# Value and gate projections of the second layer as seven block products instead of eight

## What is computed

```python
def odd_layer(x, w_in, w_gk2, b_gk, g_norm, w_out):
    h = x @ w_in                                  # (1024, 1024) @ (1024, 3088)
    q, k, v, gk_low, g = _split(h, ODD_SPLITS)    # 512, 512, 1024, 16, 1024
    o = gla_layer(q, k, v, gk_low, w_gk2, b_gk, g_norm) * jax.nn.silu(g)
    return o @ w_out
...
x = layer_norm(DEEPNORM_ALPHA * x + y, ln_g[layer], ln_b[layer])
```

## Time and profile before

| | |
|---|---|
| median of three runs | 904.2 us (903.74 to 906.98) |
| profiled execution | 907.0 us, of which the profile's span is 905.3 |
| TensorE busy | 870.0 us (96%), 4456 matmuls |
| VectorE busy | 473.1 us (52%) |
| ScalarE busy | 283.5 us (31%) |
| GpSimd busy | 253.7 us (28%) |
| moved by DMA | 55.8 MB |

### The profile page before, as it was taken

The page is one execution under the profiler, slowest core; times in us unless marked ns, Lnnn a source line. Parts: engine busy times, 40 slices in busy tenths (PEclk is TensorE's granted clock), DMA queues, the critical chain, the costliest instruction groups (busy, mean ns, idle before and its releaser), DMA issues. The chain is left out here.

```text
span 905.3 us, 12067 instructions
## 1 busy us (share of the span) xinstructions
PE 870.0 (96%) x4456; PEld 708.6 (78%) x4456; DVE 473.1 (52%) x805; ACT 283.5 (31%) x554; POOL 253.7 (28%) x275
## 2 busy tenths in 40 slices
PE   7999999999899999999997999999999999999995
PEld 5889877766677877787875888888888888888884
DVE  5988698556787786637852634000000127545553
ACT  6251514653234334412324453001102145211220
POOL 2000001424211202307655430133323323232243
PEclk9999999999999999999998999999999999999998
DMA  9110165210000201033314110211011332121111
GB/s 326 39 28 20 47 116 103 60 55 1 1 2 1 70 2 47 1 117 113 119 69 142 47 47 0 63 55 47 12 36 47 96 126 82 42 76 47 46 58 60
DMA packets 35050, 55.80 MB, mean 62 GB/s; under 512 B 7744, under 2 KB 21312, under 8 KB 34976
## 3 DMA queue, kind: packets, MB, share of 16 engines
q1 hardware_dynamic: 34992, 55.03, 20.2%
HBM read 43.94 MB, written 9.44 MB: 59 GB/s over the span
## 5 line engine op out<-in xcount | busy, mean ns | idle before, releaser
L1596 DVE SCALAR_TENSOR_TENSOR w_out_lo<-w_out_raw,vecs,w_out_hi 128x1024 fp32r<-128x1024 f32 x8 | 10.3, 1285 | 162.0 <-ACT w_out_hi L1186 161.8
L1887 PEld LDWEIGHTS psum<-V,probT 128*128 128x128 f32 x576 | 69.3, 192 | 12.5 <-issue 8.6
L1887 PE MATMUL psum<-V,probT 128*128 128x64 f32 x576 | 74.5, 275 | 0.5 <-DVE rot L1539 0.3
L1750 PE MATMUL psum<-kT,qTt 96*128 96x512 f32 (+3 forms) x192 | 72.9, 490 | 1.2 <-DVE YT L626 1.2
L1101 ACT ACTIVATE prob<-psum,negmax 128x128 f32<-128x128 f32 (+7 forms) x64 | 47.4, 741 | 82.1 <-DVE negmax L1478 74.4
L1478 DVE TENSOR_REDUCE negmax<-psum 128x1 f32<-128x128 f32 (+7 forms) x64 | 48.5, 758 | 29.5 <-PE psum L1754 28.0
L1663 PE MATMUL psum<-x1T_hi,wqk_hi 128*128 128x512 f32 x128 | 51.0, 398 | 0.0
L1663 PE MATMUL psum<-x1T_lo,wqk_hi 128*128 128x512 f32 x128 | 50.8, 397 | 0.0
L1663 PE MATMUL psum<-x1T_hi,wqk_lo 128*128 128x512 f32 x128 | 50.8, 397 | 0.0
L1663 PE MATMUL psum<-w_out_hi,Y1T_hi 128*128 128x512 f32 x128 | 50.6, 395 | 0.0
L1663 PE MATMUL psum<-w_out_hi,Y1T_lo 128*128 128x512 f32 x128 | 49.9, 390 | 0.0
(11 more groups left out here) (360 smaller groups left out, 2046.0 us busy)
## 6 DMA issues: line engine op xcount, KB each, us to landing
wqk_raw<-odd_w_in_dram SPq DMA_DIRECT2D x8, 512.0 KB, 5.4
x_res<-x_dram SPq DMA_DIRECT2D x8, 512.0 KB, 4.2
x_scratch<-zn SPq DMA_DIRECT2D x8, 512.0 KB, 2.9
wv_raw<-odd_w_in_dram SPq DMA_DIRECT2D x16, 256.0 KB, 2.7
wg_raw<-odd_w_in_dram SPq DMA_DIRECT2D x16, 256.0 KB, 2.7
w_out_raw<-odd_w_out_dram SPq DMA_DIRECT2D x4, 1024.0 KB, 4.9
V<-x_scratch SPq DMA_DIRECT2D x8, 512.0 KB, 4.2
out_dram<-SG SPq DMA_DIRECT2D x8, 512.0 KB, 2.9
```

The source lines that it names most:

```text
L1596: step(vec.scalar_tensor_tensor(w_out1[2][:, k, :], w_out1[0][:, k, :], gla_c[:, 4 + k % 2:5 + k % 2], w_out1[1][:, k, :].bitcast(F32), AL ...
L1750: mm = pe.matmul(psum[:, slot + part, 0:c1 - c0], qTt[:, i % 2, h, :], kT[:, h, c0:c1], start=True, stop=not diag, skip_group_check=diag)
L1887: mm = pe.matmul(bank("o", i)[:, h * VD:(h + 1) * VD], lhsT, rhs, start=(k == 0), stop=(k == len(pairs) - 1))
```

## The change

v1 and g1 become seven products of half-size blocks each, by Strassen's identity in the form with few additions. The 1024 tokens and 1024 channels of the input and the channels and columns of the weights are cut in halves. A11 and A12 multiply input blocks by plain weight blocks and gather in one bank; the other five (S2, S3, A22, S1, S4) take sums and differences of input blocks or of weight blocks. One product of one of v1 and g1 is 4 channel blocks ("slices") x 4 token tiles x 3 matmuls of the same shape as before; there are 56 slices, numbered 0 to 55, v1 and g1 in turn for each product. For each slice 1 to 4 pieces of 256 KB are loaded (`PIECES`) into one of three slots, and GpSimd and VectorE subtract them: two pieces GpSimd alone, three GpSimd then VectorE, four GpSimd twice, then VectorE. ScalarE makes the hi part, VectorE the lo part; only the first four slices are still split by GpSimd.

The sums of input blocks (`sum_raw`, `s2_raw`, `x1_lo_raw`) are made once: six instructions of 2048 columns on GpSimd, three after k1 of m = 5 and three after k1 of m = 7, and 16 of 512 columns on VectorE; ScalarE and VectorE split them again. The products are put together in V1 and SG: ScalarE copies A11 and A11 + A12 out, VectorE adds the other five onto it, and Silu runs in place on ScalarE. VectorE and ScalarE have a list of 60 rounds ("tick"), one per slice and four behind. `w_out1` is loaded and split in halves of 512 columns, the load of `ln_gb` is moved behind the stage, and its place is used by one of the slots. The memset of `att` moves into round 46, and the two semaphores of the output stores become one.

The core of the diff:

```diff
+        sum_raw = at("sum_raw", RD + 4096, [P, 4, 512])
...
+        vg_raw = [[at(f"vg{s}_raw{j}", a, [P, 512]) for j, a in enumerate(slot[:4])] for s, slot in enumerate(vg_at)]
+        vg_hi = [at(f"vg{s}_hi", slot[4], [P, 512], F32R) for s, slot in enumerate(vg_at)]
+        vg_lo = [at(f"vg{s}_lo", slot[5], [P, 512], F32R) for s, slot in enumerate(vg_at)]
...
+        A11, A12, S2, S3, A22, S1, S4 = range(7)
+        PIECES = {A11: ((0, 0),), A12: ((1, 0),), S2: ((1, 1), (0, 1), (0, 0)), S3: ((1, 1), (0, 1)),
+                  A22: ((1, 0), (1, 1), (0, 1), (0, 0)), S1: ((0, 1), (0, 0)), S4: ((1, 1),)}
+        ADDS_TO = (A12, A22, S4)
+        NVG = 56
+
+        for product in range(7):
+            for name in ("v1", "g1"):
+                for t in range(4):
+                    ring(name, product, t)
...
+        def vg_slice(n):
+
+            step_, k = divmod(n, 4)
+            return step_ // 2, ("v1", "g1")[step_ % 2], k
...
+        first_rows, last_rows = slice(0, 512), slice(512, S)
+        row_parts = {A11: (slice(0, 4), first_rows), A12: (slice(4, 8), first_rows), S3: (slice(0, 4), last_rows),
+                     A22: (slice(4, 8), last_rows), S1: (slice(4, 8), first_rows), S4: (slice(0, 4), first_rows)}
...
+        ROW_SUMS = (S2, S3, S1, S4)
...
+            def vg_load(n):
+
+                if n >= 7:
+                    sp.wait_ge(vg_split, n - 6)
+                product, name, k = vg_slice(n)
+                base = {"v1": 2 * GKW, "g1": c_gk + GR}[name]
+                for j, (r, c) in enumerate(vg_pieces(n)):
+                    sp.dma_start(vg_raw[n % 3][j][:, :], w_in1[r * 512 + k * P:r * 512 + (k + 1) * P,
+                                                               base + c * 512:base + (c + 1) * 512]).then_inc(
+                        vg_loaded[n % 3], 16)
...
+            plan.filled(sp, ("k1", 2 * GH - 1))
+            sp.wait_ge(qk_set, 2 * GH)
+            for n in range(4, NVG):
+                vg_load(n)
+                if n == 45:
+                    plan.filled(sp, ("g1", A22, 3))
+                    w_out1_load(0, 0, 1)
+                    w_out1_load(0, 4, 1)
+                if n == 53:
+                    plan.filled(sp, ("g1", S1, 3))
+                    w_out1_load(1, 4, 0)
+            plan.filled(sp, ("g1", S4, 3))
+            w_out1_load(2, 0, 0)
+            for n, w in enumerate((ln_g, ln_b)):
+                sp.dma_start(ln_gb[:, n, :], w[1:2, :].partition_broadcast(P)).then_inc(ln1_loaded, 16)
...
+            plan.filled(pool, ("k1", 5))
+            upper, lower = (slice(None), slice(0, 4), last_rows), (slice(None), slice(4, 8), last_rows)
+            step(pool.tensor_tensor(sum_raw[:, :, :], x1T_hi[upper].bitcast(F32), x1T_hi[lower].bitcast(F32), ALU.add))
+            step(pool.tensor_tensor(s2_raw[:, :, :], x1T_lo[upper].bitcast(F32), x1T_lo[lower].bitcast(F32), ALU.add))
+            step(pool.tensor_tensor(sum_raw[:, :, :], sum_raw[:, :, :], s2_raw[:, :, :], ALU.add), s1_s3_set)
+
+            plan.filled(pool, ("k1", 2 * GH - 1))
+            corner = (slice(None), slice(0, 4), first_rows)
+            step(pool.tensor_tensor(x1_lo_raw[upper], x1T_lo[corner].bitcast(F32), x1T_lo[upper].bitcast(F32), ALU.subtract))
+            step(pool.tensor_tensor(x1_hi_raw[upper], x1T_hi[corner].bitcast(F32), x1T_hi[upper].bitcast(F32), ALU.subtract))
+            step(pool.tensor_tensor(x1_lo_raw[upper], x1_lo_raw[upper], x1_hi_raw[upper], ALU.add), s1_s3_set)
+
+            for n in range(4, NVG):
+                q, *p = [raw[:, :] for raw in vg_raw[n % 3]][:len(vg_pieces(n))]
+                if p:
+                    pool.wait_ge(vg_loaded[n % 3], vg_landed(n))
+                if len(p) == 1:
+                    step(pool.tensor_tensor(q, q, p[0], ALU.subtract), vg_pool_sum)
+                elif len(p) == 2:
+                    step(pool.tensor_tensor(p[0], p[0], p[1], ALU.subtract), vg_pool_sum)
+                elif len(p) == 3:
+                    step(pool.tensor_tensor(p[1], p[1], p[2], ALU.subtract))
+                    step(pool.tensor_tensor(p[0], p[0], p[1], ALU.subtract), vg_pool_sum)
...
+            def vg_round(n):
+
+                if n >= 7:
+                    vg_done(act, n - 3)
+                if len(vg_pieces(n)) == 1:
+                    act.wait_ge(vg_loaded[n % 3], vg_landed(n))
+                elif len(vg_pieces(n)) == 2:
+                    act.wait_ge(vg_pool_sum, vg_pool_sums(n))
+                else:
+                    act.wait_ge(vg_vec_sum, vg_vec_sums(n))
+                step(act.activation(vg_hi[n % 3][:, :], vg_raw[n % 3][0][:, :], ACT.Copy), vg_hi_set)
...
+            def product_out(name, product, t):
+
+                job, dst = (name, product, t), {"v1": V1, "g1": SG}[name]
+                if product in (A11, A12):
+                    plan.filled(act, job)
+                    cols = first_rows if product == A12 else last_rows
+                    step.frees(act.activation(dst[:, t, cols], bank(*job),
+                                              ACT.Silu if name == "g1" and product == A12 else ACT.Copy), job)
+                elif name == "g1" and product in (A22, S1, S4):
+                    plan.drained(act, job)
+                    z = {A22: SG[:, 4 + t, first_rows], S1: SG[:, 4 + t, last_rows], S4: SG[:, t, last_rows]}[product]
+                    step(act.activation(z, z, ACT.Silu))
...
+            for tick in range(2, NVG + 4):
+                if tick + 2 < NVG:
+                    vg_round(tick + 2)
+                for first, product in ((8, S2), (17, S3), (21, S1), (25, S4)):
+                    if first <= tick < first + 4:
+                        rows_round(product, tick - first)
+                if tick >= 4:
+                    product, name, t = vg_slice(tick - 4)
+                    product_out(name, product, t)
+                if 48 <= tick < 56:
+                    w_out1_hi(tick - 48, 1)
+                if 56 <= tick < 60:
+                    w_out1_hi(tick - 52, 0)
...
+            def vg_low(n):
+
+                vec.wait_ge(vg_hi_set, n - 3)
+                step(vec.tensor_tensor(vg_lo[n % 3][:, :], vg_raw[n % 3][0][:, :], vg_hi[n % 3][:, :].bitcast(F32),
+                                       ALU.subtract), vg_split)
+
+            def vg_sum(n):
+
+                if len(vg_pieces(n)) >= 3:
+                    vec.wait_ge(vg_pool_sum, vg_pool_sums(n))
+                    q, p = vg_raw[n % 3][0][:, :], vg_raw[n % 3][1][:, :]
+                    step(vec.tensor_tensor(q, q, p, ALU.subtract), vg_vec_sum)
...
+            def product_sum(name, product, t):
+
+                job, dst = (name, product, t), {"v1": V1, "g1": SG}[name]
+                if product in (A11, A12):
+                    return
+                plan.filled(vec, job)
+                if product == S2:
+                    plan.drained(vec, (name, A11, t))
+                right, below = dst[:, t, last_rows], dst[:, 4 + t, last_rows]
+                out_, with_ = {S2: (right, right), S3: (below, right), A22: (dst[:, 4 + t, first_rows], right),
+                               S1: (below, below), S4: (right, right)}[product]
+                ins = vec.tensor_tensor(out_, with_, bank(*job), ALU.add)
+                step.frees(ins, job)
+
+            vec.wait_ge(s1_s3_set, 1)
+            for tick in range(NVG + 4):
+                if 4 <= tick + 2 < NVG:
+                    vg_low(tick + 2)
+                if 4 <= tick + 3 < NVG:
+                    vg_sum(tick + 3)
+                if tick < 4:
+                    k = tick
+                    step(vec.tensor_tensor(s2_raw[:, k, :], sum_raw[:, k, :], x1T_hi[:, k, first_rows].bitcast(F32), ALU.subtract))
+                    step(vec.tensor_tensor(s2_raw[:, k, :], s2_raw[:, k, :], x1T_lo[:, k, first_rows].bitcast(F32), ALU.subtract),
+                         s2_s4_set)
+                if 8 <= tick < 12:
+                    k = tick - 8
+                    if k == 0:
+                        plan.filled(vec, ("g1", A11, 3))
+                        vec.wait_ge(s1_s3_set, 2)
+                    s4 = x1_lo_raw[:, k, first_rows]
+                    step(vec.tensor_tensor(s4, x1T_hi[:, 4 + k, first_rows].bitcast(F32), s2_raw[:, k, :], ALU.subtract))
+                    step(vec.tensor_tensor(s4, s4, x1T_lo[:, 4 + k, first_rows].bitcast(F32), ALU.add), s2_s4_set)
+                for first, product in ((12, S2), (17, S3), (21, S1), (25, S4)):
+                    if first <= tick < first + 4:
+                        rows_low(product, tick - first)
+                if tick >= 4:
+                    product, name, t = vg_slice(tick - 4)
+                    product_sum(name, product, t)
+                if tick == 46:
+                    step(vec.memset(att[:, :, :, :], 0.0))
+                if 49 <= tick < 57:
+                    w_out1_lo(tick - 49, tick - 49, 1)
+                if 57 <= tick < 60:
```

(31 more changed lines are left out.)

164 lines of the change are left out of this document (83 added, 81 removed).

## The result

The changed kernel takes 921.4 us (median of four runs, 919.03 to 926.27) against 904.2 us before: ratio 1.0188, 95% interval 1.0125 to 1.0251. It is slower; whether by more than 2% the interval leaves open. A fourth run of the kernel before, in the same session, fell in a slow state (992.4 us) and is not counted. The profiled execution took 919.03 us, its span 917.0, against 907.0 and 905.3.

What follows compares the result with a forecast made beforehand. It took TensorE, busy throughout the value and gate projections, as the bound; −21.8 + 5.6 + 2.5 + 4.0 + 9.8 + 2.7 = +2.8 us gave 909.8 profiled, 907.0 median. Likeliest case 897 to 916; 8-in-10 range 892 to 918.

Steps and rivals of the forecast that it cites:

- step 1: Start of the stage: TensorE waits at slice 4 for VectorE's low part, held by wide GpSimd sums; 5.6 us.
- late starts in the stage: Matmuls at low clock behind the wait at slice 4: one fall to 1.2 GHz, 2.5 us.
- step 2: Products S2 and S3: VectorE's rounds 13 to 28 take longer than TensorE's slices, partly covered; 4.0 us.
- step 3: Product A22, four pieces per slice: GpSimd and VectorE strictly in turn, 3.95 us per slice against 2.72; 9.8 us.
- step 4: End of the stage: ScalarE and VectorE pass gate tiles between them, so key-value matmuls start later; 2.7 us.
- B: Rival: the clock falls again in A22 and stays at 1.2 GHz, 9.4 us more, 916 us; chance 0.12.
- S3's second condition: Start of S3: its first matmuls also need the last S2 product sum; no separate size given.
- load chain: A22: a slot is loaded again only after its low part, 10.1 us for three slices, 3.4 each.
- A: Rival: the shared port decides less, GpSimd subtracting in VectorE's pauses; 890 to 898, say 894 us; chance 0.21.
- C: Rival: GpSimd–VectorE hand-overs cost instead of saving, A22 at 5.0 us per slice; 919 us; chance 0.08.
- D: Rival: the stage isn't shortened, matmuls coming further apart with four banks sharing a slice; chance 0.02.
- high end: Whole kernel: all added costs at their upper bounds, 33.8 us, giving 916 us.

Runs made afterwards that it cites:

- e1: Changed kernel with GpSimd's six wide sums of input blocks each made as four of 512 columns: 914.7 us, ratio 1.0100.
- e7: e1 with VectorE's eight subtractions on the rows of S2 made four rounds later: 911.4 us, ratio 1.0055.
- e2: Changed kernel with GpSimd's subtractions of weight pieces on 8 of 512 columns, weights wrong: 903.7 us, ratio 0.9967.
- e8: Changed kernel with the edits of e7, e4, e6 and e5 together: 901.5 us, ratio 0.9938.
- e10: e8 with the subtractions of weight pieces back on GpSimd: 905.2 us, ratio 0.9992.
- e11: e9 with most pieces in slices 19–23 and 35–39 loaded once VectorE's piece sum is done, not after its low part: 908.6 us, ratio 1.0055.
- e9: Changed kernel with each GpSimd subtraction of weight pieces replaced by three memsets, about as long but reading nothing: 915.0 us, ratio 1.0100.
- e5: Changed kernel with all subtractions of weight pieces moved from GpSimd to VectorE: 919.4 us, ratio 1.0133.
- e3: Changed kernel loading one piece per slice instead of up to four, except in six slices; weights partly stale: 913.0 us, ratio 1.0067.
- e12: Changed kernel with only the earlier piece loads of e11: 918.6 us, ratio 1.0147.
- e4: Changed kernel with two 1 MB loads of w_out1 issued after slices 47 and 49 instead of ahead of slice 46: 918.8 us, ratio 1.0129.
- e6: Changed kernel with four half-width w_out1 parts made after the first token tile's outputs, four more after the second's: 917.4 us, ratio 1.0120.

## Why the prediction was wrong

It said slower as the likeliest sign, with 907.0 us and a range up to 918; 921.4 came, 14.4 us more. The mechanism held in most parts, but three things failed. The clock was priced as one fall; it fell four times. The loads of `w_out1` ahead of slice 46 stood at nothing; they cost 2.8 us. And I took the new median 2.8 us below the profiled run, as it was before the change; it was 2.4 above, which is 5.2 of the 14.4 us. The profiled runs account for the other 9.2:

| step | predicted | measured |
|---|---|---|
| matmuls removed | −21.8 | −21.8 |
| step 1, wait at slice 4 | +5.6 | +7.2 |
| late starts in the stage | +2.5 | +5.7, of it 4.3 by the low clock |
| step 2, S2 and S3 | +4.0 | +3.0 |
| step 3, A22, waits alone | +9.8 | +8.1 |
| slices 46 and 52 | 0 | +3.3 |
| step 4, tail | +2.7 | +3.8, and +1.5 by the clock |
| sum | +2.8 | +10.8, and some 1 us not placed: 12.0 |

**Step 1: right in size and cause, by a path that I had partly missed.** I let VectorE's two copies of `ends` run freely, since they read one operand. They took 4.14 and 3.20 us, and held back VectorE's last instructions of the queries and keys, set down for 572.6, until 579.8. The low part of slice 4 ended 1 us later than I said (587.8 instead of 586.8). e1 and e7 show that the width of GpSimd's sums and the rows' place in VectorE's order were the cause.

**The clock: a step that failed.** I priced one fall, at 2.5 us, and made a second one in A22 a rival (B, 0.12). The one behind slice 4 cost 1.2 us, less than I said. But it came twice more, in slices 33 and 37 (granted 0.87 of full speed from 672 to 698 us). It did not stay low for all of A22, so it cost 3.1 us there, not B's 9.4. A fourth one hit the key-value matmuls, 1.5 us. Over all runs the late starts go only loosely with the waits: 2.0 to 4.8 us where the waits come to 10 to 15 (e2, e8, e10, e11), 3.2 to 7.5 where they come to more. So I have no price for a wait that would hold.

**The median.** Of the three longer runs of the changed kernel only a lower mean granted clock is known. That the clock's falls vary from run to run would fit, but isn't shown.

**Step 2: right, and shown.** 3.0 us of waits at slice 24, which vanish when GpSimd reads nothing (e9) or next to nothing (e2). 2.5 of them are for the banks of S2's product sums, which the prediction had named as S3's second condition. With the weight sums on VectorE (e5, e8) 2.1 us stay there: then VectorE's own work is too much.

**Step 3: the size right, the cause half.** Eight slices took 33.9 us; I had said about 31, 3.95 us each from the alternation alone, and had called the load chain "a second, weaker limit" of 3.4 us a slice. e9 and e3 show that it wasn't weaker. With no exclusion at all the slices take 32.1 us; with short loads 28.9; e11's earlier loads bring 4.3 us, of which 1.6 are waits and the rest is clock. The two limits are one: each turn of GpSimd and VectorE lies inside the buffer's round, where the alternation lengthens it (12.0 to 13.2 us; 11.0 to 12.2 in e9). For the changed kernel as it is this is argued, since e12 doesn't settle it. I should have summed the round with the alternation in it and with 1 MB in four pieces in 6.3 us, not the single 1 MB in 4.9 of the earlier trace rows. One thing the sum had no place for: 7.0 of the 8.1 us of waits in A22 are not for low parts but for banks that a product sum frees, at the third and fourth token tile of slice 32 and the fourth of slice 36. VectorE comes to that sum after the piece sum in its order, so what delays the one delays the other; no run parted them.

**Slice 46: the missing term.** For S1 and S4 the prediction says only that TensorE keeps its pace, and it counts `w_out1`'s loads at the end of the stage alone. SyncE issues 2 MB of them ahead of weights that are due in 8 us: 2.8 us, gone in e4 and e3. The 0.5 us at slice 52 are something else, a bank that a product sum frees; they are in every run, 0.5 to 1.0 us.

**Step 4: right in cause, 1.1 us short**, and the clock on top. e6 takes away 2.4 of the 3.8 us and the clock's 1.5.

**The rivals.** A (the port decides less than I reckon, 894) is false: GpSimd's reads had to go to free slices 16 to 31 of waits (e9), and even that kernel took 915.0 us. C (hand-overs cost instead of saving) is false too: 1.70 us per pair in e1 is 0.28 us less than 1.29 + 0.69. No pause of 0.115 us shows there either; the section of the Trainium skill that the prediction cites has that figure from GpSimd's descriptor writes behind a VectorE copy, so I had carried it over to another case. D is false: the spacing stayed 0.227 us. B's condition came twice, its price did not.

My high end needs a word. 916 for the median was 919 for the profiled run, and 919.0 is what that run took. All costs at their upper bounds came to 33.8 us, and so did the measured ones, but by luck: steps 2 and 3 took 11.1 us where the bounds had 21.2, and that room was filled by what the bounds left out, slices 46 and 52, falls of the clock beyond the first, a longer step 1 and tail, and small gaps. What put the median beyond the range is its distance from the profiled run.

## What to carry to other kernels

Removing matmuls pays only as far as the engines that feed TensorE keep its pace: write down for each buffer the whole round, from its release over load, each engine's turn and each exclusion to the next release, and compare it with TensorE's time for as many slices as there are buffers. A subtraction given to GpSimd is no relief for a VectorE that reads two SBUF operands; do it on VectorE if it costs less there than the exclusion (0.69 against 1.29 us here). Look in SyncE's order at what is ahead of each load that is due soon, and keep large loads out of stretches with little slack. Look also at what TensorE waits for, tile by tile: here nearly half of the waiting was for a bank to be emptied, so the place of the emptying instruction in its engine's order is a thing to try. And forecast the median and the profiled run apart.

## What the hardware showed

- **A VectorE copy of eight columns waits for GpSimd.** With one SBUF operand it took 4.14 us beside a GpSimd sum of 2048 columns, and 0.17 in the earlier trace rows; beside sums of 512 columns in e1 0.64. I had looked at the number of operands alone. The Trainium skill, "SBUF — State Buffer", section "Who interferes with whom", has this case: copies can, under conditions, enter a mode that takes the shared port pair too. The trace agrees in that the copy waited until GpSimd's end; which mode it ran in no run shows. The prediction had left that sentence out.
- **It is GpSimd's reads that exclude.** Low parts took 0.93 us on average beside subtractions and 0.70 beside memsets about as long into the same buffers (e9). The same section states that a VectorE instruction with two SBUF inputs contends with a GpSimd instruction that reads SBUF and not with one that only writes; this run agrees.
- **The alternation is strict and a little cheaper than the sum**: 1.70 us per pair of 0.69 and 1.29.
- **256 KB took up to 9.7 us to land** behind 2 MB issued before it, where the median is 2.7 in the earlier trace rows.
